# RWKV scan: the backward direction's tokens on the other half of the partitions, Gram products of both directions together

## What is computed

```python
def rwkv7_scan(r, w, k, v, kk, a, s0):
    def step(s, inp):
        rt, wt, kt, vt, kkt, at = inp
        sa = jnp.einsum('nbhij,nbhj->nbhi', s, kkt)
        s = (s * wt[..., None, :] - sa[..., :, None] * (kkt * at)[..., None, :]
             + vt[..., :, None] * kt[..., None, :])
        return s, jnp.einsum('nbhij,nbhj->nbhi', s, rt)
    xs = tuple(jnp.moveaxis(t, 2, 0) for t in (r, w, k, v, kk, a))
    s_fin, y = lax.scan(step, s0, xs)
    return jnp.moveaxis(y, 0, 2), s_fin
```

## Time and profile before

| what | value |
|---|---|
| three runs | 4488.19, 4491.84, 4509.91 us |
| median | 4491.84 us |
| span of the profiled execution | 4487.5 us (its own time is not listed apart) |
| busy, share of the span | TensorE 90%, weight loads 60%, VectorE 47%, GpSimd 27%, ScalarE 26% |
| scan stage | about 1410 to 2610 us |

### The profile page before, as it was taken

One profiled execution on the slowest core, in us unless ns is written; L12 is line 12 of the kernel. 1 busy time (PEld: TensorE's weight loads), 2 busy tenths in 40 slices (PEclk: granted clock), 3 DMA queues, 4 the chain that ended last, 5 costly groups with the idle time before them and its releaser, 6 DMA issues. The chain is left out here.

```text
span 4487.5 us, 104862 instructions
## 1 busy us (share of the span) xinstructions
PE 4020.4 (90%) x40634; PEld 2714.7 (60%) x40634; DVE 2103.7 (47%) x3818; ACT 1154.2 (26%) x2839; POOL 1208.9 (27%) x1508
## 2 busy tenths in 40 slices
PE   5999969999997899999999958785999999999987
PEld 3777847666765789888888834444333333433333
DVE  2111156777674566666666648884111111111116
ACT  1000034443443344344344423320000000000000
POOL 0000011111010354454554534433222222222220
PEclk9999989999998999999999979886999999999999
DMA  9521156556555433432443354433566999999987
GB/s 285 217 69 60 51 163 200 192 196 196 188 182 167 129 126 97 137 128 93 139 130 92 101 175 143 134 108 134 217 262 256 378 403 395 401 398 420 420 359 309
DMA packets 328746, 925.40 MB, mean 206 GB/s; under 512 B 73480, under 2 KB 170952, under 8 KB 279616
## 3 DMA queue, kind: packets, MB, share of 16 engines
q1 hardware_dynamic: 274544, 772.02, 48.0%
q0 software_dynamic: 46928, 131.38, 8.2%
q10 hardware_dynamic: 6912, 16.78, 1.0%
HBM read 969.46 MB, written 208.53 MB: 263 GB/s over the span
## 5 line engine op out<-in xcount | busy, mean ns | idle before, releaser
L2676 PE MATMUL exp_gate_up<-exp_w_gate,exp_rows_and_rowsT 128*64 128x512 f32 x1664 | 730.1, 595 | 13.8 <-DMA exp_w_up<-in_moe_w_up_dram 12.7
L2676 PE MATMUL exp_gate_up<-exp_w_up,exp_rows_and_rowsT 128*64 128x512 f32 x1664 | 730.6, 595 | 0.0
L2676 PEld LDWEIGHTS exp_gate_up<-exp_w_gate,exp_rows_and_rowsT 128*64 128x64 f32 x1664 | 227.3, 138 | 480.8 <-issue 480.8
L823 PE MATMUL rwp_product<-rwp_hT,rwp_w_rw 128*128 128x256 f32 (+1 forms) x1936 | 422.6, 381 | 0.3 <-DVEq L766 0.3
L2627 DVE TENSOR_TENSOR exp_hidden<-exp_hidden,exp_gate_up 64x512 f32<-64x512 f32 x104 | 71.9, 692 | 700.1 <-ACT exp_hidden L2608 689.7
L823 PEld LDWEIGHTS rwp_product<-rwp_hT,rwp_w_rw 128*128 128x128 f32 (+1 forms) x1936 | 362.8, 188 | 58.4 <-issue 0.7
L1000 PE MATMUL hgp_product<-hgp_hT,const_w_hg 128*128 128x256 f32 x1664 | 380.8, 384 | 12.8 <-DVEq L981 12.8
L2701 PE MATMUL exp_down<-exp_w_down,exp_hiddenT 128*64 128x512 f32 x1664 | 380.0, 597 | 3.7 <-issue 0.7
L1000 PEld LDWEIGHTS hgp_product<-hgp_hT,const_w_hg 128*128 128x128 f32 x1664 | 314.7, 192 | 65.7 <-DVEq L981 15.4
L2608 ACT ACTIVATE exp_hidden<-exp_gate_up 64x512 f32<-64x512 f32 x104 | 61.3, 589 | 952.4 <-PE exp_gate_up L2676 952.4
L2585 POOL DMA_INDIRECT s_yb<-exp_out,exp_row_slot x104 | 105.0, 1009 | 568.6 <-PE exp_rows_turned L2661 443.0
(11 more groups left out here) (418 smaller groups left out, 7143.2 us busy)
## 6 DMA issues: line engine op xcount, KB each, us to landing
exp_w_gate<-in_moe_w_gate_dram SPq DMA_DIRECT2D x208, 1024.0 KB
exp_w_up<-in_moe_w_up_dram SPq DMA_DIRECT2D x208, 1024.0 KB
exp_w_down<-in_moe_w_down_dram SPq DMA_DIRECT2D x104, 2048.0 KB
s_rw_in<-prep_operands SPq DMA_DIRECT2D x72, 514.0 KB, 4.1
rw_operands<-s_rw_in SPq DMA_DIRECT2D x72, 514.0 KB, 8.0
hg_qkf<-s_hg_in SPq DMA_DIRECT2D x36, 768.0 KB, 9.4
rw_tokens<-s_rw_tm SPq DMA_DIRECT2D x144, 192.0 KB, 4.9
const_w_hg<-in_w_mod_dram SPq DMA_DIRECT2D x24, 1024.0 KB, 17.8
```

Source lines behind the costliest of these rows:

```text
L823: mm = nc.tensor.matmul(mp[o % 2][0:width, 0:GROUP], w_in[:, k, c0 - 5 * D_HG:c0 - 5 * D_HG + width], hT[b][:, k, :], start=(k == 0), stop ...
L2676: i = nc.tensor.matmul(pgu[u][q:q + BLK], xT[:, k, r * BLK:(r + 1) * BLK], w[r][:, k, :], start=(k == 0), stop=(k == KD - 1))
```

## The change

Tokens of the backward direction of head half h lie on the other half of the partitions (`tokens_at`); channels stay where they are. For d = 1 the products from channels to tokens (grams, alpha and rho by state) and from tokens to channels (state) go through the two quarters off the diagonal, the products from tokens to tokens stay on it. A gram entry issues both directions at once, head pair by head pair, in all four quarters, and waits first for both directions' masks and rows. The sums of `rhs` and `out` for d = 1 have sources in different quarters; they are issued in two parts, with the forward direction between them and a wait on a semaphore (`rhs_half`, `y_half`) ahead of the second part. The readout reads the backward y with its head axis reversed.

```diff
+def tokens_at(d, h):
+
+    return HALF[h ^ d]
...
-                sp.dma_start(self.tm[v][d][h * RW_C:(h + 1) * RW_C].rearrange("s x j e -> s x (j e)"), tok[h]).then_inc(got, 16)
+                sp.dma_start(self.tm[v][d][tokens_at(d, h)].rearrange("s x j e -> s x (j e)"), tok[h]).then_inc(got, 16)
...
-        def rhs(d, v, c):
-            s = self.s[d]
+        def rhs_state(v, c):
+
+            s, al, o = self.s[1], self.part(self.ch[v][1], "alpha"), self.pb[1]
+            wait(pe, s["s_ready"], c)
+            wait(pe, s["y_ready"], c - RW_CTX)
+            pe.wait_ge(s[f"chain_loaded{v}"], 48 * m)
             if isinstance(c, int) and c == 0:
                 pe.wait_ge(self.zeroed, 1)
+            pe.sem_inc(self.turns, 1)
+            for j in range(NPAIR):
+                for h, q in enumerate(HALF):
+                    i = nc.tensor.matmul(o[tokens_at(1, h), 0, j, :], al[q, j, :], self.st[1][q, j, :], start=(j == 0), stop=False,
+                                         skip_group_check=True)
+            i.then_inc(s["rhs_half"], 1)
+
+        def rhs_tokens(v, c):
+            s, kk, tm, o = self.s[1], self.kk[w][1], self.tm[v][1], self.pb[1]
+            pe.wait_ge(s["masked"], 4 * m)
+            pe.wait_ge(s["rhs_half"], c + 1)
+            pe.sem_inc(self.turns, 1)
+            for j in range(NPAIR):
+                for q in HALF:
+                    i = nc.tensor.matmul(o[q, 0, j, :], kk[q, v, j, 0, :], tm[q, 2, j, :], start=False, stop=(j == NPAIR - 1), skip_group_check=True)
+            i.then_inc(s["rhs_psum"], 1)
+
+        def rhs(v, c):
+            rhs_state(v, c)
+            s = self.s[0]
...
+            rhs_tokens(v, c)
...
-        def out(d, v, c):
-            s = self.s[d]
+        def out_state(v, c):
+
+            s, rho, o = self.s[1], self.part(self.ch[v][1], "rho"), self.pb[1]
             pe.wait_ge(s["u_ready"], c + 1)
             pe.sem_inc(self.turns, 1)
...
+            for j in range(NPAIR):
+                for h, q in enumerate(HALF):
+                    i = nc.tensor.matmul(o[tokens_at(1, h), 0, j, :], rho[q, j, :], self.st[1][q, j, :], start=(j == 0), stop=False,
+                                         skip_group_check=True)
+            i.then_inc(s["y_half"], 1)
+
+        def out_tokens(v, c):
+            s, o = self.s[1], self.pb[1]
+            pe.wait_ge(s["y_half"], c + 1 - RW_CTX)
...
             i.then_inc(s["y_psum"], 1)
+
+        def out(v, c):
+            out_state(v, c)
+            s = self.s[0]
+            pe.wait_ge(s["u_ready"], c + 1)
...
+            i.then_inc(s["y_psum"], 1)
+            out_tokens(v, c)
...
-        def gram(d, k, v):
...
+        def gram(k, v):
+
+            for d in range(2):
+                s = self.s[d]
+                if k == 0:
+                    pe.wait_ge(s[f"row_loaded{v}"], 16 * m + 16)
+                if k == 0 and v == 0:
+                    wait(pe, s["r_ready"], 6 * m)
+                else:
+                    pe.wait_ge(s["masked"], 4 * m + 2 * k + v)
             pe.sem_inc(self.turns, 1)
...
+            for j in range(NPAIR):
+                for d in range(2):
+                    row = self.row[v][d]
+                    left = self.part(row, "beta" if k == 0 else "kappa")
...
+                    for h, c in enumerate(HALF):
+                        q = tokens_at(d, h)
+                        if full:
+                            i = nc.tensor.matmul(dst[q, j].rearrange("p x t -> p (x t)"), left[c, j, :], both[c, :, j, :], start=True, stop=True)
...
+                    if j == NPAIR - 1:
+                        i.then_inc(self.s[d]["grams"], 1)
...
+        backward = natural(self.y[u][1])[:, :, ::-1, :]
...
-        o.link(V.tensor_tensor(yn[:].rearrange("p (j h e) -> p j h e", j=NPAIR, h=2), natural(self.y[u][0]), natural(self.y[u][1]), ALU.add))
+        o.link(V.tensor_tensor(yn[:].rearrange("p (j h e) -> p j h e", j=NPAIR, h=2), natural(self.y[u][0]), backward, ALU.add))
```

More of the change, by code:

```diff
@@ L1518, in rhs @@
             pe.sem_inc(self.turns, 1)
[L1519 removed]
+            al, kk, tm, o = self.part(self.ch[v][0], "alpha"), self.kk[w][0], self.tm[v][0], self.pb[0]
             for j in range(NPAIR):
[L1521 to L1523 removed]
+                for q in HALF:
+                    nc.tensor.matmul(o[q, 0, j, :], al[q, j, :], self.st[0][q, j, :], start=True, stop=False)
+                for q in HALF:
                     i = nc.tensor.matmul(o[q, 0, j, :], kk[q, v, j, 0, :], tm[q, 2, j, :], start=False, stop=True)
             i.then_inc(s["rhs_psum"], 1)
+            rhs_tokens(v, c)
         def solve(d, v, c):
@@ new lines, in out_tokens @@
+        def out_tokens(v, c):
+            s, o = self.s[1], self.pb[1]
+            pe.wait_ge(s["y_half"], c + 1 - RW_CTX)
+            pe.sem_inc(self.turns, 1)
+            for j in range(NPAIR):
+                for q in HALF:
+                    nc.tensor.matmul(o[q, 0, j, :], self.kk[w][1][q, v, j, 1, :], self.tm[v][1][q, 2, j, :], start=False, stop=False,
+                                     skip_group_check=True)
+                for q in HALF:
+                    i = nc.tensor.matmul(o[q, 0, j, :], self.ar[w][1][q, v, j, 1, :], self.uu[1][q, j, :], start=False, stop=(j == NPAIR - 1),
+                                         skip_group_check=True)
+            i.then_inc(s["y_psum"], 1)
@@ new lines, in out @@
+        def out(v, c):
+            out_state(v, c)
+            s = self.s[0]
+            pe.wait_ge(s["u_ready"], c + 1)
+            pe.sem_inc(self.turns, 1)
+            rho, o = self.part(self.ch[v][0], "rho"), self.pb[0]
+            for j in range(NPAIR):
+                for q in HALF:
+                    nc.tensor.matmul(o[q, 0, j, :], rho[q, j, :], self.st[0][q, j, :], start=True, stop=False)
+                for q in HALF:
+                    nc.tensor.matmul(o[q, 0, j, :], self.kk[w][0][q, v, j, 1, :], self.tm[v][0][q, 2, j, :], start=False, stop=False)
+                for q in HALF:
+                    i = nc.tensor.matmul(o[q, 0, j, :], self.ar[w][0][q, v, j, 1, :], self.uu[0][q, j, :], start=False, stop=True)
+            i.then_inc(s["y_psum"], 1)
+            out_tokens(v, c)
@@ L1558, in state @@
             for j in range(NPAIR):
-                for _, q in heads[0:2]:
-                    nc.tensor.matmul(o[q, 1, j, :], tm[q, 1, j, :], tm[q, 2, j, :], start=True, stop=False)
-                for _, q in heads[0:2]:
-                    i = nc.tensor.matmul(o[q, 1, j, :], tm[q, 0, j, :], self.uu[d][q, j, :], start=False, stop=True)
-            i.then_inc(s["s_psum"], 1)
-        def gram(d, k, v):
-            s = self.s[d]
-            if k == 0:
-                pe.wait_ge(s[f"row_loaded{v}"], 16 * m + 16)
-            if k == 0 and v == 0:
-                wait(pe, s["r_ready"], 6 * m)
-            else:
-                pe.wait_ge(s["masked"], 4 * m + 2 * k + v)
-            pe.sem_inc(self.turns, 1)
-            row = self.row[v][d]
-            left = self.part(row, "beta" if k == 0 else "kappa")
-            both = row[:, 0:2 * XW].rearrange("p (x j t) -> p x j t", x=2, j=NPAIR)
-            dst = self.pa[d][:].rearrange("p a b t -> p (a b t)").rearrange("p (j x t) -> p j x t", j=NPAIR, x=2)
-            for j, q in heads:
-                if full:
-                    i = nc.tensor.matmul(dst[q, j].rearrange("p x t -> p (x t)"), left[q, j, :], both[q, :, j, :], start=True, stop=True)
-                else:
-                    i = nc.tensor.matmul(dst[q, j, 0, :], left[q, j, :], both[q, 0, j, :], start=True, stop=True)
-            i.then_inc(s["grams"], 1)
@@ L1605, in pe @@
             for v in range(2):
-                for name, f in chain.items():
-                    if name != "state" or v == 0:
-                        f(0, v, 2 * m - 2 + v)
-                        f(1, v, 2 * m - 2 + v)
+                c = 2 * m - 2 + v
+                rhs(v, c)
+                solve(0, v, c)
+                solve(1, v, c)
+                out(v, c)
+                if v == 0:
+                    state(0, v, c)
+                    state(1, v, c)
             return
@@ L1616, in pe @@
                     c = 2 * m - 2 + v
-                    if with_output(m, 1) and (kind != "out" or with_output(c, RW_CTX)):
+                    if not with_output(m, 1) or kind == "out" and not with_output(c, RW_CTX):
+                        continue
+                    if kind in ("solve", "state"):
                         chain[kind](d, v, c)
+                    elif d == 0:
+                        chain[kind](v, c)
                 elif name[:-2] == "gram":
-                    gram(d, int(name[-2]), v)
+                    if d == 0:
+                        gram(int(name[-2]), v)
                 else:
```

24 lines of the change are left out of this document (12 added, 12 removed).

## The result

The changed kernel takes 4522.8 us (median of 4 runs, 4515.36 to 4524.77); the kernel before, run beside it, 4490.01 us (4 runs, 4487.25 to 4509.91). The ratio is 1.0058, interval 1.0037 to 1.0079: slower by 33 us. The forecast was 4518 us, slower.

The account below looks back on a forecast made before the run. TensorE and ScalarE were taken to arrive nearly together at `out_a`. 15 x (0.42 + 1.4) = 27.3, first full couple -1, end +3, X copies -2.8: +26.5 on 4491.84 gives 4518 us; 8-in-10 range 4489 to 4534.

Parts of the forecast that it names:

- The wait: Ahead of `out_a`: TensorE stops about 3.9 us a couple until ScalarE copies u of the backward direction.
- The Gram slots: In the scans: each slot of 32 Gram records takes 0.93 us in place of 1.75 us.
- Rival 2: Gram products are no quicker because quarters above each other take turns; 4510 us, chance 0.12.
- Rival 3: Four quarters slow each other to 3.5 us a Gram slot, +3 us a couple; 4537 us, chance 0.07.
- The new order of `out`: In `out_a`: all 96 records come after the wait for the backward u, ending 1.40 us later.
- The clock: Behind each stop of 3.9 us: one stretch of low clock, 1.4 us a couple, bounds 0 and 2 us.
- Rival 1: The clock doesn't fall, or recovers during the stop; 4497 us, chance 0.14.
- The two terms: Per couple, in 15 couples: 0.42 us later start of the item behind `gram1b`, plus 1.4 us of low clock.
- the X copies: Behind `gram1b`: TensorE's waits for these copies, 2.8 us in 15 times, would vanish.
- The waits on own sums: At `rhs_half` and `y_half`: 48 records behind their source, costing nothing, at worst 0.2 us x 2 in each chunk.
- The end: Last couple and a half, with no other work beside the chain: the order costs +3 us (0 to 5).
- Rival 4: The stop lets instructions catch up, ending 43.9 us of idle on "issue"; all of it 4463 us, chance 0.09.

Follow-up runs that it names:

- two_quarters: Changed kernel with Gram products issued per direction again, forward before backward, backward tokens staying in their changed places: 4532.91 us, ratio 1.0089.
- before_wait_both: Kernel before, with only a wait for the backward u added ahead of both directions' `out`: 4514.65 us, ratio 1.0056.
- filled: Changed kernel with 40 products (80 records) of no use put into the stop ahead of `out_a`: 4509.56 us, ratio 1.0038.
- fwd_first: Changed kernel with `out` of the forward direction issued first, ahead of the backward direction's two parts: 4504.12 us, ratio 1.0024.
- late_q: early_u with GpSimd reordered as well: forward k, two levels, backward k, and the scalings of q late in the couple: 4475.10 us, ratio 0.9971.
- before_late_q: Kernel before with the same two altered orders of ScalarE and GpSimd as late_q: 4474.77 us, ratio 0.9978.
- early_u: Changed kernel with both u copies of the first chunk moved ahead of ScalarE's second table load and exponentials: 4521.11 us, ratio 1.0057.

## Why the prediction was right

**The wait** is as forecast: ahead of `out_a`, ended by ScalarE's u, in all 15 couples. I gave 3.9 us; it is 3.51 us. Of the 0.4 us, 0.22 are a wait for the masks of `gram0a` that I had not seen; the rest lies at `solve`, which waits 0.23 us for the rhs copies and takes 1854.03 - 1852.85 = 1.18 us to the next start. The rhs copies have not the microsecond in hand that I gave them. The second u copy kept its distance, 9.37 us.

**The Gram slots** were given 0.93 us each and take 0.94. Rival 2, that they are no quicker, is out by these rows, and so is the form in which I had thought of undoing it: `two_quarters` shows that the place of the tokens alone brings about half of it (1.42 us a slot, between 1.80 and 0.94). Rival 3 is out as well.

**The new order of `out`** was priced at +1.40 us. `before_wait_both` has it alone, and it is 1.40 us wherever the clock stays up. In the changed kernel it is 1.23 us (`filled`), because `out` itself is 0.17 us shorter there.

**The clock** was given 1.4 us a couple, with bounds 0 and 2. In the couple shown, `out_a` takes 4.95 us and the score behind it 0.96, where `filled` has 2.77 and 0.61 us: 2.53 us. In the mean of 14 couples it is 1.76 us, since in most of them the clock comes back sooner. I had put the low clock on the `gram1b`; it lies on `out_a`, which is over before. That a price read behind another wait, on other products, came within 0.4 us is in part luck. Rival 1, that it doesn't fall, is out: the low clock over the whole couple rises by 2.21 us, and `filled`, which removes about half of the low clock, is faster by it.

**The couple.** The two terms, 0.42 + 1.4 less 0.19 for the X copies, gave +1.63 us. Measured: part a +2.99, `gram1b` itself -1.02 (1865.60 - 1864.56 = 1.04 in place of 2.06), all else -0.16: +1.81 us. The sum came closer than its terms: the order was booked too high, the clock too low, and the shorter `rhs_b`, `out_b` and `state`, which I had put at nothing, are offset by more idle time and low clock behind `gram1b`.

**Smaller terms.** The 2.8 us of waits for the X copies were to vanish and did not: the row is there with the same 2.8. A delay of the whole couple does not relax a wait between two engines that are both delayed by it. The waits on own sums cost nothing where other records stand between, 48 for `y_half` and 32 for `rhs_half` (not 48, as I wrote), and 3.6 us where none do (`fwd_first`). The first full couple, booked at -1 us, takes 65.7 us in place of 67.1. The end, booked at +3 us beside the last full couple, is 6.6 us, some 4.8 us without that couple's 1.8; 0.7 us of it is a stop on "issue". The reversed operand of the readout costs nothing, as booked:

```profile
L2114 DVE TENSOR_TENSOR read_y_sum<-read_rw_y x16: 681/693/1426, 2653.4 to 3026.0; 128x512 f32<-128x512 f32 x16
```

**Rival 4**, that the stop lets instructions catch up, is wrong: the four rows on "issue" make 48.6 us after, and 43.9 before. That what a stop holds ahead is used long before the next stops, as the text against it said, fits this but was not tried by itself.

What the prediction had not asked is what the change would be worth with its stop removed. It booked three of the four slots as lost to ScalarE and would have given them back with ScalarE's order mended, some 2.6 us a couple. `late_q` against `before_late_q` shows they are not. Under ScalarE's order lies GpSimd's: `early_u` and `late_q` show that. Under GpSimd's lie the stops on "issue"; that these are a supply of instructions is argued from the packets alone.

## What to carry to other kernels

Work taken from an engine pays only up to the next input it waits for: read when that input comes, and what its own engine does up to then, before pricing the saving. Look then at what the edit queues behind that wait; here an order that was harmless while both inputs came together moved 1.4 us of products behind the later one, and the stop cost 1.8 us more in clock. And before keeping a faster form, give the old one the same mended order: the gain here was all in the orders of ScalarE and GpSimd.

## What was unexpected of the hardware

- Gram products of both directions in four quarters take 0.94 us in place of 1.80, over both row halves of one column half. If one direction is issued wholly behind the other they still overlap in part: 1.42 us.
- After a stop of 3.51 us, products of 29 ns a record went at 52 ns at a granted clock of 0.50, in 4 of 15 couples to the end of their 96 records (4.95 us), in the others for a part of them (3.95 to 4.32 us); 2.53 us of idle products in that stop kept it at 1.00. By the Trainium skill, "TensorE: Matmul & The Clock Gate", section Part 1: The HAM clock gate, the clock follows how busy the array has been of late; the trace agrees, also with products whose result nobody reads.
- A stop of 1.89 us (`before_wait_both`), about half as long, brought a low clock in only 3 of 15 couples, and not at once: in the couple shown the groups behind it ran at 0.31 us for over a microsecond, and then at 0.48 us.
- TensorE's stops without a visible reason end about 2.5 us behind the start of a 16 KB packet of instructions, under full DMA engines and (in `late_q`) under idle ones.
- GpSimd's product of 128x256 takes 0.72 to 0.74 us in most cases but 1.28 us in the row of `early_u` above; of 128x512 1.27 us or 1.74. Which other work slows it was not tried.
